# A dot product's second input moves to PSUM, and VectorE's and GpSimd's work is put in another order

## What is computed

```python
q = (ht @ w_q).reshape(T, PEER_HEADS, 2, PEER_DKEY // 2)        # 8 heads, 2 halves
s = jnp.einsum('thpd,pnd->thpn', q, sub_keys)                   # 128 keys a half
top_s, top_i = lax.top_k(s, 16)
cand_s = top_s[:, :, 0, :, None] + top_s[:, :, 1, None, :]      # 16 x 16 sums
best_s, best_pos = lax.top_k(cand_s, 16)                        # 16 experts of 16384 a head
g = jax.nn.softmax(best_s, axis=-1)
act = jax.nn.gelu(jnp.einsum('cd,chkd->chk', xc, u_experts[ic]), approximate=False)
out = jnp.einsum('chk,chkd->cd', gc * act, v_experts[ic])
```

## Time and profile before

| what | us |
|---|---|
| median of 3 runs | 2100.16 (2097.12 to 2106.31) |
| profiled execution, its own time | 2099.87 |
| its span, first to last instruction | 2098.0 |
| `phase_experts`, about 803 to 1546 of the span | 743 |
| of it, ranking stretch with dots, 911 to 1217 | 306 |
| of it, gate stretch, 1245 to 1541 | 296 |

### The profile page before, as it was taken

One profiled execution on the slowest core, in us unless ns is written; L12 is line 12 of the kernel. 1 busy time (PEld: TensorE's weight loads), 2 busy tenths in 40 slices (PEclk: granted clock), 3 DMA queues, 4 the chain that ended last, 5 costly groups with the idle time before them and its releaser, 6 DMA issues. The chain is left out here.

```text
span 2098.0 us, 28277 instructions
## 1 busy us (share of the span) xinstructions
PE 1880.0 (90%) x10096; PEld 1630.3 (78%) x10096; DVE 1587.1 (76%) x2260; ACT 729.5 (35%) x970; POOL 789.7 (38%) x487
## 2 busy tenths in 40 slices
PE   4999789999899798978787878899969999999998
PEld 4888666777679688878777778888858888888886
DVE  6444365553446588989999889999958888887887
ACT  3222234443323222322222245555534333333331
POOL 0000293000140003579687876666632332333320
PEclk7999989999999899999999999999989999999999
DMA  8754123333661523679999989999989999999991
GB/s 284 261 180 140 45 76 91 91 91 105 214 228 41 103 61 83 156 213 286 243 277 248 257 222 287 276 277 275 285 298 385 381 386 370 357 357 354 368 349 74
DMA packets 312737, 475.96 MB, mean 227 GB/s; under 512 B 16426, under 2 KB 239451, under 8 KB 311132
## 3 DMA queue, kind: packets, MB, share of 16 engines
q1 hardware_dynamic: 275804, 340.89, 54.3%
q0 software_dynamic: 36864, 134.23, 18.9%
HBM read 413.71 MB, written 60.82 MB: 226 GB/s over the span
## 5 line engine op out<-in xcount | busy, mean ns | idle before, releaser
L117 PE MATMUL u_s<-h_hi,u_hi 128*128 128x384 f32 x1024 | 357.2, 349 | 72.9 <-POOL u_lo L1502 67.4
L1502 POOL TENSOR_TENSOR u_lo<-u_ut,u_hi 128x1024 fp32r<-128x1024 f32 x127 | 320.4, 2523 | 175.7 <-ACT u_hi L1526 175.0
L119 PE MATMUL u_s<-h_hi,u_lo 128*128 128x384 f32 x1024 | 346.5, 338 | 0.0
L118 PE MATMUL u_s<-h_lo,u_hi 128*128 128x384 f32 x1024 | 346.5, 338 | 0.0
L117 PE MATMUL v_o<-v_v_hi,v_w_hi 128*128 128x512 f32 x768 | 299.9, 391 | 16.8 <-DVE v_w_lo L1938 15.6
L118 PE MATMUL v_o<-v_v_lo,v_w_hi 128*128 128x512 f32 x768 | 299.5, 390 | 0.0
L119 PE MATMUL v_o<-v_v_hi,v_w_lo 128*128 128x512 f32 x768 | 299.5, 390 | 0.0
L117 PEld LDWEIGHTS u_s<-h_hi,u_hi 128*128 128x128 f32 x1024 | 195.2, 191 | 91.7 <-issue 40.3
L1877 ACT ACTIVATE v_v_hi<-v_raw 128x1024 fp32r<-128x1024 f32 x128 | 127.5, 1051 | 338.0 <-PE v_o L119 275.6
L1583 DVE CUSTOM_DVE_ANT_0 rows_buf<-rows_buf,u_ht 128x1024 f32<-128x1024 f32 x128 | 215.9, 1697 | 12.5 <-DMA rows_buf<-in_u_experts_dram,few_idx 12.5
L1904 DVE TENSOR_TENSOR v_v_lo<-v_raw,v_v_hi 128x1024 fp32r<-128x1024 f32 x128 | 149.5, 1220 | 86.2 <-ACT v_v_hi L1877 85.9
(11 more groups left out here) (308 smaller groups left out, 3648.9 us busy)
## 6 DMA issues: line engine op xcount, KB each, us to landing
u_raw<-in_u_experts_dram SPq DMA_DIRECT2D x256, 256.0 KB, 6.4
v_raw<-in_v_experts_dram SPq DMA_DIRECT2D x128, 512.0 KB, 5.8
expert_acts<-u_ao SPq DMA_DIRECT2D x64, 384.0 KB, 4.2
expert_gates<-u_gs SPq DMA_DIRECT2D x12, 2048.0 KB, 7.5
v_gt<-expert_gates SPq DMA_DIRECT2D x32, 768.0 KB, 14.7
w_in_raw<-in_w_in_dram SPq DMA_DIRECT2D x17, 1024.0 KB, 5.5
proj_ada<-in_w_ada_dram SPq DMA_DIRECT2D x8, 2048.0 KB, 8.4
gate_w_raw<-in_w_in_dram SPq DMA_DIRECT2D x32, 512.0 KB, 4.0
```

Of the source, the lines that this page charges most:

```text
L117: nc.tensor.matmul(out, w[0], x[0], start=first, stop=False)
L118: nc.tensor.matmul(out, w[0], x[1], start=False, stop=False)
L119: return nc.tensor.matmul(out, w[1], x[0], start=False, stop=last)
L1502: nc.gpsimd.tensor_tensor(lo[j][:, :, :], ut[j][:, :, :], hi[j][:, :, :].bitcast(F32), ALU.subtract).then_inc(sem["lo_ok"], 1)
```

## The change

Four edits, all in `phase_experts`:

1. `ht` goes from SBUF to PSUM (`p_h`, two banks); the dot products read it there. To make room `p_s` shrinks from four banks to two, so that product(t) waits for gelu(t - 2) where it waited for gelu(t - 4).
2. In the gate stretch VectorE's order becomes match(g), dot, transpose of tile 80 + g + 2, hot(g).
3. split_lo(t) gets one more wait. In the ranking stretch it waits until VectorE has done all ranking steps that stand ahead of `transposes(t + 1)` (`quiet`). In the gate stretch it waits for match(t - 1 - 80).
4. GpSimd's program is written after VectorE's, and its loop over tiles 2 to 19 is unrolled.

```diff
-        ht = k.sb("ht", [P, D])
-        p_s = [k.ps(f"s{j}", [P, S]) for j in range(4)]
+        p_s = [k.ps(f"s{j}", [P, S]) for j in range(2)]
         p_g = [k.ps(f"g{j}", [P, 4, P]) for j in range(4)]
+        p_h = k.ps("h", [P, D])
...
+        quiet = {}
...
             def split_lo(t, j, wait=True):
                 pool.wait_ge(sem["hi_ok"], t + 1)
+                if isinstance(t, int) and t + 1 in quiet:
+                    pool.wait_ge(sem["step"], quiet[t + 1])
+                if isinstance(t, int) and PLAIN <= t - 1 < TILES - 2:
+                    pool.wait_ge(sem["hot_ok"], 2 * (t - 1 - PLAIN) + 1)
                 if wait:
                     pool.wait_ge(sem["mm"], t - 1)
...
-            with pool.Fori(1, KNOWN_AT // 2) as i:
-                for j in range(2):
-                    split_lo(2 * i + j, j)
+            for t in range(2, KNOWN_AT):
+                split_lo(t, t % 2)
...
-                nc.scalar.activation(ht[:, :].rearrange("p (q m r) -> p m q r", q=4, m=KD)[:, 4 * j:4 * j + 4],
+                nc.scalar.activation(p_h[:, :].rearrange("p (q m r) -> p m q r", q=4, m=KD)[:, 4 * j:4 * j + 4],
...
-                nc.vector.tensor_tensor_reduce(out=row, in0=row, in1=ht[:, :], scale=1.0, scalar=0.0, op0=ALU.mult, op1=ALU.add,
+                nc.vector.tensor_tensor_reduce(out=row, in0=row, in1=p_h[:, :], scale=1.0, scalar=0.0, op0=ALU.mult, op1=ALU.add,
...
                 if spent[0] >= gap:
+                    quiet[tile[0]] = steps.n
                     transposes(tile[0])
...
                 nc.vector.tensor_tensor(m[:, :, :, :].rearrange("p s t (y x) -> p (s t) y x", x=2), index, key, ALU.is_equal).then_inc(sem["hot_ok"], 1)
+                if PLAIN + g + 2 < TILES:
+                    transposes(PLAIN + g + 2)
                 dve.wait_ge(sem["hot_ok"], 2 * g + 1)
...
                 nc.vector.tensor_tensor(h[:, :, :, :].rearrange("p s t (y x) -> p s t y x", x=2), ones, w, ALU.mult).then_inc(sem["hot_ok"], 1)
-                if PLAIN + g + 2 < TILES:
-                    transposes(PLAIN + g + 2)
...
-                    pe.wait_ge(sem["act_ok"], t - 3)
+                    pe.wait_ge(sem["act_ok"], t - 1)
                 for c in range(KD):
-                    ins = three(nc, p_s[j][:, 0:NT], (hi[j % 2][:, c, :], lo[j % 2][:, c, :]),
+                    ins = three(nc, p_s[j % 2][:, 0:NT], (hi[j % 2][:, c, :], lo[j % 2][:, c, :]),
```

More of the change, by code:

```diff
@@ L1532, in gelu @@
                     act.wait_ge(sem[f"a_out{j // 2}"], (t - j) * 4)
-                nc.scalar.activation(ao[j // 2][:, j % 2, :], p_s[j][:, 0:NT], ACT.Gelu).then_inc(sem["act_ok"], 1)
+                nc.scalar.activation(ao[j // 2][:, j % 2, :], p_s[j % 2][:, 0:NT], ACT.Gelu).then_inc(sem["act_ok"], 1)
             def plain(i, first=False):
@@ L1726, in _, with split_lo, fetch @@
                 nc.vector.tensor_tensor(h[:, :, :, :].rearrange("p s t (y x) -> p s t y x", x=2), ones, w, ALU.mult).then_inc(sem["hot_ok"], 1)
-                if PLAIN + g + 2 < TILES:
-                    transposes(PLAIN + g + 2)
             for n in range(dots_by(TILES - 1), NSLOT):
                 dot(n)
+        @block.gpsimd
+        def _(pool):
+            nc.gpsimd.iota(upto[:, :, :], pattern=[[1, TOPK], [0, P]], base=0, channel_multiplier=0,
+                           allow_small_or_imprecise_dtypes=True).then_inc(sem["iota_ok"], 1)
+            nc.gpsimd.iota(iota[:, :], pattern=[[1, P]], base=0, channel_multiplier=0,
+                           allow_small_or_imprecise_dtypes=True).then_inc(sem["iota_ok"], 1)
+            def split_lo(t, j, wait=True):
+                pool.wait_ge(sem["hi_ok"], t + 1)
+                if isinstance(t, int) and t + 1 in quiet:
+                    pool.wait_ge(sem["step"], quiet[t + 1])
+                if isinstance(t, int) and PLAIN <= t - 1 < TILES - 2:
+                    pool.wait_ge(sem["hot_ok"], 2 * (t - 1 - PLAIN) + 1)
+                if wait:
+                    pool.wait_ge(sem["mm"], t - 1)
+                nc.gpsimd.tensor_tensor(lo[j][:, :, :], ut[j][:, :, :], hi[j][:, :, :].bitcast(F32), ALU.subtract).then_inc(sem["lo_ok"], 1)
+            def fetch(n):
+                if n >= RING:
+                    pool.wait_ge(sem["dot_ok"], n - RING + 1)
+                gather_rows(nc, rows[n % RING][:, :], a["u_experts"], few["idx"], n).then_inc(row_in[n % RING], 16)
+            pool.wait_ge(sem["lo_ok"], 1)
+            split_lo(1, 1, False)
+            for t in range(2, KNOWN_AT):
+                split_lo(t, t % 2)
+            pool.wait_ge(sem["known"], 1)
+            for t in range(KNOWN_AT, TILES):
+                split_lo(t, t % 2)
+                for n in range(rows_by(t - 1), rows_by(t)):
+                    fetch(n)
         @block.tensor
@@ L1746, in plain @@
                 for j in range(4):
-                    product(4 * i + j, j, not first)
+                    product(4 * i + j, j, not (first and j < 2))
             plain(0, True)
```

## The result

The changed kernel takes 2143.82 us (median of 4 runs, 2140.73 to 2145.71) against 2102.36 for the kernel before on the same chip: ratio 1.0198, 95% interval 1.0167 to 1.0229. Forecast were 2073 us, faster. The profiled execution has a span of 2138.9 us, 40.9 more than before.

A forecast was written before the change was run, and what follows sets the result against it. The prediction took VectorE to set the pace in the ranking and gate stretches, with DMA bounding ranking after the change. From 2099.87 us, -26 - 4 - 2 + 5 = -27 gave 2073 us, range 2039 to 2101.

The forecast's parts named there:

- Ranking and softmax stretches: Before the gate stretch: gains of 26 us in ranking (DMA-bound), 4 in the early stretch, 2 in softmax.
- The dot beside lo: Dot with ht in PSUM beside GpSimd's low part: not held, taken at 1.22 us.
- DMA gives way: Rival, ranking stretch: tiles go at the engines' 4.4 us, -60 in place of -26, 2039 us; chance 0.10.
- DMA is at its end already: Rival, ranking stretch: 261 GB/s stays, no gain there, 2099 us; chance 0.10.
- The p_s banks and the unrolled loop at nothing: Taking two banks from p_s and unrolling GpSimd's loop: no cost for either.
- GpSimd's waits: Ranking stretch: lo starts beside the next tile's dots and transpose, so short held steps mostly go; no separate size.
- The gate stretch: Gate stretch, new order and waits: 5 us lost (3 to 8), period 6.45 us against 6.34.
- That closes a loop over two tiles: Gate stretch: hot, product, gelu, hi, lo, transpose, hot form a loop of 12.82 us for two tiles.
- T is 6.41 to 6.50: Gate stretch: period per tile from the two-tile loop, upper end if GpSimd waits for match; 6.45 us taken.
- The fourth rival: PSUM dot held like the SBUF one: no ranking gain, gate period 7.0 us, 2131 us; chance 0.06.
- The second: Rival, gate stretch: loop does not bind, TensorE's 5.7 us a tile, 30 us gained, 2038 us; chance 0.05.
- The 8 us more: All 128 dots: estimated extra VectorE time from a PSUM source's 62 more fixed cycles, 8 us.

The follow-up runs named there:

- x1: Changed kernel with VectorE's gate-stretch order put back to match, hot, dot, transpose: 2069.19 us, ratio 0.9869 to the kernel before.
- x2: Changed kernel with SyncE issuing the next raw pair ahead of the activation and gate stores in the gate stretch: 2075.79 us, ratio 0.9891.
- x7: Changed kernel with raw loads ahead of the stores and a third transpose buffer, both in the gate stretch: 2044.44 us, ratio 0.9718.
- x9: Changed kernel with the third transpose buffer alone, raw loads still behind the stores: 2124.39 us, ratio 1.0103.
- x10: Changed kernel with loads first and a third transpose buffer, but VectorE's old gate order (match, hot, dot, transpose): 2067.26 us, ratio 0.983.
- x4: Kernel before with only ht moved to PSUM (two p_s banks), old order, no new waits: 2065.99 us, ratio 0.9843.
- x11: x7 with loads issued ahead of the activation stores in the ranking stretch too: 2046.76 us, ratio 0.9733 to the kernel before.
- x5: Kernel before with only GpSimd's two new waits and its unrolled loop, ht in SBUF, old order: 2086.56 us, ratio 0.9915.
- x8: Changed kernel with each gate store cut to a sixteenth (128 KB for 2 MB), single run: gate period 6.53 us; total of 2112.02 us not counted.
- x3: Kernel before with only the new gate-stretch order (match, dot, transpose, hot), ht in SBUF, no new wait: 2154.08 us, ratio 1.027.

## Why the prediction was wrong

**Ranking and softmax stretches: right.** Forecast were -26, -4 and -2, in all -32; the first match came 35.1 us earlier. By parts: the first dot came 5.4 us earlier (906.96 for 912.35), from there to the first operation of the softmax it took 272.1 us for 301.9, and from that to the first match 22.5 in both. The first operation of the softmax, before and after:

```profile
1214.24 0.69 DVE L1690 TENSOR_REDUCE u_z<-few_sel 128x32 f32<-128x512 f32 x1 [4.74 <-ACT few_sel L1551]
1179.02 0.69 DVE L1663 TENSOR_REDUCE u_z<-few_sel 128x32 f32<-128x512 f32 x1 [4.44 <-ACT few_sel L1523]
```

In x1, x2, x7, x9 and x10, the same code up to there, the first match stands at 1202.4 to 1206.2, so a few of the 35 us are scatter. The dot beside lo was 1.18 to 1.22 us, as the operation of the earlier trace rows had led me to expect. DMA did become the bound, at 292 GB/s where I had taken 285; x4 has 291, x7 288 and x11 284. "DMA gives way" and "DMA is at its end already" both fell.

**The p_s banks and the unrolled loop at nothing: right** as far as x4 tells, which has the two banks and is the fastest version in the old order, and x5, which has the unrolled loop.

**GpSimd's waits: half right.** They were to save the short held steps. Without the PSUM dot they do save time (x5), but for the most part in the dots. Beside a PSUM dot VectorE is busy 219 us of the ranking stretch's 275 with them and 223 without (x4), but the stretch is as long, since DMA bounds it.

**The gate stretch: wrong, by 70 us, and this is the step that failed:** "That closes a loop over two tiles", and with it "T is 6.41 to 6.50". The loop is real and was sized well (6.44 in x2, 6.53 in x8). But I followed only one of the two things for which `transposes` waits, lo. The other, the raw rows, closes a longer loop: store of activations, load behind it on SyncE, landing, transpose, hot, gate matmuls, product, gelu, store, over four tiles. The prediction has no term for the raw rows in this stretch: in the kernel before VectorE waited for them once, 0.9 us. That was not slack. In the turn shown they landed 0.4 us ahead, and no row of SyncE's timeline had been laid beside VectorE's. The term of the edit was +5; it measured +75.

On top come two consequences that I had not priced. After the stall lo and hot fall together, so hot is held for 1.5 us. And while TensorE stood idle from about 1412.3 to 1417.9, its granted clock fell from full speed (2.4 GHz) to half (1.2 GHz); it was at half from 1417 to 1423 and at full from 1424:

```profile
1410.00:1416.00 6.00, 2.26 (x14) 1.94 (x12) 2.59 (x2) 1.43 (x2) 3.14 (x2) 1.00 0.95 282
1417.00:1423.00 6.00, 5.10 (x32) 5.11 (x33) 6.00 (x7) 2.17 (x2) 1.60 (x1) 0.50 0.81 195
1424.00:1430.00 6.00, 6.00 (x52) 5.84 (x52) 1.11 (x2) 3.44 (x4) 2.35 (x1) 1.00 0.00 0
```

So gate matmuls and product take 8.2 us instead of 5.8. An estimate from this turn: 33.0 - 1.5 - 2.4 leaves 29.1 us for four tiles, 7.3 a tile, still well over the 6.4 of the two-tile loop, so the late rows would have set the pace without them too. How much of the 75 us the clock and the held hot make was not tried apart.

**The fourth rival** (a held PSUM dot) did not come true, but its mechanism and nearly its price did in x3, with the SBUF dot. **The second** (the gate loop does not bind, 2038) did not come true either: both waits do bind. Only x7, which opens the loop, came near its time with 2044.

## What to carry to other kernels

When an operation is moved ahead of the one that the bottleneck waits for, list all that it waits for, DMA included, and follow each back to where it closes on itself, through the issuing engine's queue too. A transfer that is hardly ever waited for may be on time by 0.4 us: lay its issue beside its use before you lengthen what depends on it. A move that made the kernel 2% slower was worth 1% in the other direction, once its loads were issued ahead of the stores and one buffer was added.

## What the runs showed of the hardware

The dot with one input in PSUM took no longer than a free one with both in SBUF: the shortest of 128 was 1.18 us in either kernel, the longest 1.22 in the changed one. There 28 of the 128 dots ran wholly inside a low part of GpSimd's, and none was held. The 8 us more that the prediction had estimated from the Trainium skill, "VectorE: DVE Perf Modes", section on the TRN2 errata, did not show.

SyncE took 4.1 to 4.8 us to issue the four loads of a pair behind a gate store of 2 MB in the changed kernel's gate stretch, and 1.9 to 2.3 otherwise. With the store at 128 KB (x8) it took 1.9 to 2.1 behind it too. So a large store delays even the issuing of the loads that follow it on the same queue.

In the changed kernel GpSimd's gather took 0.96 us beside the transpose. When it began at 1416.30, beside hot, which reads two SBUF inputs and lasted to 1417.77, it took 2.30:

```profile
1403.60 0.96 POOL L1191 DMA_INDIRECT rows_buf<-in_u_experts_dram,few_idx  x1
...
1416.30 2.30 POOL L1191 DMA_INDIRECT rows_buf<-in_u_experts_dram,few_idx  x1
```
